# One more radix-2 step in the Fourier group's token transform, and another order of steps 11 to 14 and of the end of the heads

## The reference

```python
h = layer_norm(x, ln_in_g, ln_in_b)
for l in range(DEPTH):
    a_q, a_k, a_v, b_u, b_b, b_c, c_u, d_q, d_k, d_v = split_columns(h @ w_in[l])
    out_a = windowed_gqa_sink(a_q, a_k, a_v, sink[l])       # window 128, ALiBi, sink
    out_b = short_conv_mixer(b_u, b_b, b_c, conv_w[l])      # width 3, gated
    out_c = fourier_mixer(c_u)                              # fft2 over tokens and head width, real part
    out_d = dense_gqa(axial_rope(rms_norm(d_q)), axial_rope(rms_norm(d_k)), d_v)
    mix = concatenate([rms_norm(o, g_i) for o in (out_a, out_b, out_c, out_d)])
    h = layer_norm(DN_ALPHA * h + mix @ w_out[l], ln1_g[l], ln1_b[l])
    h = layer_norm(DN_ALPHA * h + jnp.square(jax.nn.relu(h @ w1[l])) @ w2[l], ln2_g[l], ln2_b[l])
```

## Time and profile before

| | |
|---|---|
| median of 3 runs | 1057.16 us (1056.75 to 1057.83) |
| profiled execution | 1057.18 us, span 1055.1 us |
| TensorE busy | 1038.5 us, 98% |
| VectorE, ScalarE, GpSimd busy | 761.5, 532.4, 116.8 us |
| mean granted TensorE clock | 0.998 |
| chain of waits | TensorE 94%, GpSimd 2% |

### The profile page before, as it was taken

The page is one execution under the profiler, slowest core; times in us unless marked ns, Lnnn a source line. Parts: engine busy times, 40 slices in busy tenths (PEclk is TensorE's granted clock), DMA queues, the critical chain, the costliest instruction groups (busy, mean ns, idle before and its releaser), DMA issues.

```text
span 1055.1 us, 15201 instructions
## 1 busy us (share of the span) xinstructions
PE 1038.5 (98%) x5281; PEld 868.7 (82%) x5281; DVE 761.5 (72%) x1035; ACT 532.4 (50%) x777; POOL 116.8 (11%) x122
## 2 busy tenths in 40 slices
PE   7999999999999999999999999999999999999996
PEld 6888887988888888888888888879888888888885
DVE  7845876878668757758887558677884884785787
ACT  3433666665355255355634247666634643642654
POOL 5200343200000000000002004331000000000003
PEclk9999999999999999999999999999999999999999
DMA  8432023031521521521243410311243134125122
GB/s 292 160 120 80 1 61 121 9 121 59 187 74 40 199 80 40 174 106 53 108 144 139 160 41 22 120 42 49 80 157 122 40 124 156 40 92 186 40 80 80
DMA packets 17378, 105.47 MB, mean 100 GB/s; under 512 B 2016, under 2 KB 2704, under 8 KB 5792
## 3 DMA queue, kind: packets, MB, share of 16 engines
q1 hardware_dynamic: 15984, 98.70, 26.3%
q0 software_dynamic: 1184, 5.86, 1.7%
q10 hardware_dynamic: 144, 0.07, 0.0%
HBM read 101.49 MB, written 2.10 MB: 98 GB/s over the span
## 4 chain that ended last, share of the span: by engine, by line
PE 94%; POOL 2%; issue 1%; ACT 1%; DMA 1%; DVE 0%; DVEq 0%; SPq 0%; POOLq 0%; ACTq 0%
PE bank L465 19%; PE bank L466 18%; PE bank L467 18%; PE bank L815 9%; PE bank L814 9%; PE bank L813 9%; PE bank L753 2%; PE bank L738 2%; PE bank L474 1%; PE bank L644 1%; PE bank L645 1%; POOL w_lo L1816 1%; PE bank L541 1%; POOL x L1911 1%; PE bank L548 1%
## 5 line engine op out<-in xcount | busy, mean ns | idle before, releaser
L465 PE MATMUL bank<-h_hi,w_hi 128*128 128x512 f32 (+1 forms) x688 | 257.8, 375 | 0.0
L466 PE MATMUL bank<-h_lo,w_hi 128*128 128x512 f32 (+1 forms) x688 | 257.5, 374 | 0.0
L467 PE MATMUL bank<-h_hi,w_lo 128*128 128x512 f32 (+1 forms) x688 | 257.5, 374 | 0.0
L813 PE MATMUL bank<-w_hi,hid_hi 128*128 128x512 f32 x448 | 174.4, 389 | 0.0
L815 PE MATMUL bank<-w_hi,hid_lo 128*128 128x512 f32 x448 | 174.3, 389 | 0.0
L814 PE MATMUL bank<-w_lo,hid_hi 128*128 128x512 f32 x448 | 174.3, 389 | 0.0
L1257 DVE TENSOR_TENSOR w_lo<-w_raw,w_hi 128x2048 fp32r<-128x2048 f32 x62 | 141.8, 2287 | 39.2 <-ACT w_hi L929 32.7
L929 ACT CAST w_hi<-w_raw 128x2048 fp32r<-128x2048 f32 x56 | 107.1, 1913 | 85.8 <-PE bank L815 61.5
L466 PEld LDWEIGHTS bank<-h_lo,w_hi 128*128 128x128 f32 x688 | 129.5, 188 | 23.1
L465 PEld LDWEIGHTS bank<-h_hi,w_hi 128*128 128x128 f32 x688 | 129.5, 188 | 23.0
L467 PEld LDWEIGHTS bank<-h_hi,w_lo 128*128 128x128 f32 x688 | 129.5, 188 | 23.1
(11 more groups left out here) (184 smaller groups left out, 1610.3 us busy)
## 6 DMA issues: line engine op xcount, KB each, us to landing
w_raw<-in_weights SPq DMA_DIRECT2D x63, 1024.0 KB, 4.7
w_third<-in_weights SPq DMA_DIRECT2D x23, 1024.0 KB, 4.8
rows<-in_rows POOLq DMA_DIRECT2D x4, 1024.0 KB, 4.7
w_raw<-in_weights SPq DMA_DIRECT2D x4, 512.0 KB, 8.5
out_h<-x SPq DMA_DIRECT2D x8, 256.0 KB, 2.0
x<-in_x SPq DMA_DIRECT2D x3, 512.0 KB, 9.6
dft<-in_dft SPq DMA_DIRECT2D x2, 512.0 KB, 7.0
qk_gain<-in_qk_gain POOLq DMA_DIRECT2D x3, 192.0 KB, 3.5
```

The lines of the kernel that those rows point to most:

```text
L465: pe.matmul(dst, s_hi, m_hi, start=first, stop=False)
L466: pe.matmul(dst, s_hi, m_lo, start=False, stop=False)
L467: return pe.matmul(dst, s_lo, m_hi, start=False, stop=last)
L813: pe.matmul(bank[dst + t][:], s_hi, m_hi, start=start, stop=False, skip_group_check=goes_on)
```

## The change

Three things. First, the sums for the even frequencies are folded a second time: VectorE makes them in a buffer `even` and from it the sums and differences of token n and n + 128. The frequencies 0, 4, 8, ... then need one matmul on 128 tokens, and so do 2, 6, 10, ...; each writes every second column of the bank. The columns of the table `dft` are put in that order. Secondly, in steps 11 to 14 there is one side item in each, where there were two in 11 and two in 13; and in every step `sum_quad` comes behind `turn_probs`. Thirdly, behind the last step the order is another on TensorE, ScalarE and VectorE. GpSimd's order is as it was.

```diff
--- before.py
+++ after.py
@@ -96,10 +96,10 @@
     stats=6, moments=3, row_sum=5, neg_mean=5, row_square=5, var_ready=8, rstd=8, centred=16, normed=16, rows=32,
     param=32,
     qk_gain=TOK, qk_square=TOK, dv_copied=TOK, qk_sum=TOK, qk_eps=TOK, qk_rstd=1, qk_unit=TOK,
-    rope_cos=TOK, rope_sin=2 * TOK, qk_roped=2 * TOK, tk_copied=2 * TOK, aq_hi=4, aq_lo=4, bu_copied=2,
+    rope_cos=TOK, folded_even=1, rope_sin=2 * TOK, qk_roped=2 * TOK, tk_copied=2 * TOK, aq_hi=4, aq_lo=4, bu_copied=2,
     conv_step=8, conv_out=2, group_square=4, square_added=2, square_sum=2,
     mix_hi=12, mix_lo=10, fourier_lo=2, square_mean=10, group_rstd=10,
-    qk_turned=6, k_hi=4, k_lo=4, dq_copied=2, dq_hi=4, dq_lo=2, dq_moved=32, freq=2, freq_copied=2, mixed=2, sine_copied=2, folded=2, fourier_step=4, fourier_out=2,
+    qk_turned=6, k_hi=4, k_lo=4, dq_copied=2, dq_hi=4, dq_lo=2, dq_moved=32, freq=2, freq_copied=2, mixed=2, sine_copied=2, folded=3, fourier_step=4, fourier_out=2,
     scores=UNITS, sink_put=16, biased=16, neg_max=UNITS, probs=UNITS,
     inv_denom=8, inv_widened=8, inv_turned=8, inv_copied=8, head_out=8, out_square=8, out_square_added=8, quad_sum=8, prob_turned=UNITS, prob_copied=UNITS, attended=UNITS,
     added=4 * 8 + CHUNKS * CHUNK_ADDS, relu=32, hidden_square=32, hidden_sum=16 * CHUNKS, hidden_hi=12 * CHUNKS, hidden_lo=12 * CHUNKS,
@@ -161,9 +161,10 @@
 
 SIDE_STEPS = {-1: [("s", 0)]}
 for _g in range(3):
-    SIDE_STEPS.update({4 * _g + _t: w_items(_g, _t, _t + 1) for _t in range(TOK)})
+    SIDE_STEPS.update({4 * _g + _t: w_items(_g, _t, _t + 1) for _t in range(TOK) if (_g, _t) != (2, 3)})
 SIDE_STEPS[3] = [("s", 1)] + SIDE_STEPS[3]
-SIDE_STEPS.update({13: w_items(3, 0, 1), 15: w_items(3, 1, 2), 16: w_items(3, 2, 4)})
+SIDE_STEPS.update({11: [("w", 2, 3, 0)], 12: [("w", 2, 3, 1)], 13: [("w", 3, 0, 0)], 14: [("w", 3, 0, 1)],
+                   15: w_items(3, 1, 2), 16: w_items(3, 2, 4)})
 SIDE = sum((SIDE_STEPS[_step] for _step in sorted(SIDE_STEPS)), [])
 FIRST_OF = {}
 for _step in sorted(SIDE_STEPS):
@@ -264,6 +265,7 @@
         sqd = share("sqd", [P, 2, QK])
         rope_a = share("rope_a", [P, QK])
         rope_b = share("rope_b", [P, QK])
+        even, _ = place("even", [P, 2, GROUP], F32, at=at_sqd + 4 * 2 * QK)
         freq, _ = place("freq", [P, 2, BANK], F32, at=at_sqd)
         head_square, _ = place("head_square", [P, GROUP], F32, at=at_sqd)
         inv_rows, _ = place("inv_rows", [P, GROUP], F32, at=at_sqd + 4 * GROUP)
@@ -650,12 +652,13 @@
                         scores(0)
                         scores(1)
                     wait(pe, l, "conv_step", 4 * (ct + 1))
-                    wait(pe, l, "folded", 2)
-                    for odd in range(2):
-                        c = slice(odd * SEQ // 2, (odd + 1) * SEQ // 2)
-                        for t in range(TOK // 2):
-                            last = pe.matmul(bank[4 + ct][:, c], folded[:, 2 * odd + t, ct * P:(ct + 1) * P], dft[:, t, c],
-                                             start=(t == 0), stop=(t == TOK // 2 - 1))
+                    wait(pe, l, "folded", 3)
+                    of = slice(ct * P, (ct + 1) * P)
+                    for r in range(2):
+                        pe.matmul(bank[4 + ct][:, r:HALF - 1:2], folded[:, r, of], dft[:, 0, r * P:(r + 1) * P], start=True, stop=True)
+                    c = slice(SEQ // 2, SEQ)
+                    for t in range(TOK // 2):
+                        last = pe.matmul(bank[4 + ct][:, c], folded[:, 2 + t, of], dft[:, t, c], start=(t == 0), stop=(t == TOK // 2 - 1))
                     last.then_inc(sems["freq"], 1)
 
                 wait(pe, l, "conv_out", 2)
@@ -766,26 +769,25 @@
                         take_values(p - 2)
                     if quad_scaled_in(p) is not None:
                         turn_inverse(quad_scaled_in(p))
+                    for u in pair(p - 1):
+                        turn_probs(u)
                     if quad_high_in(p) is not None:
                         sum_quad(quad_high_in(p))
-                    for u in pair(p - 1):
-                        turn_probs(u)
                 wait(pe, l, "probs", UNITS)
                 turn_half(l, 1, 0, 0)
-                take_values(PAIRS - 2)
                 for u in pair(PAIRS - 1):
                     turn_probs(u)
-                sum_quad(6)
-
-                turn_half(l, 1, 0, 1)
-                take_values(PAIRS - 1)
-                turn_inverse(7)
                 last_sides = list(sides_of(PAIRS))
                 side(last_sides[0])
                 side(last_sides[1])
-                sum_quad(7)
+                sum_quad(6)
+                take_values(PAIRS - 2)
+                take_values(PAIRS - 1)
+                turn_inverse(7)
+                turn_half(l, 1, 0, 1)
                 turn_stream(1)
                 side(last_sides[2])
+                sum_quad(7)
                 side(last_sides[3])
 
 
@@ -1119,7 +1121,7 @@
                 for u in pair(PAIRS - 1):
                     copy_turned(u)
                 copy_inverse(7)
-                stream_high_tile(0)
+                stream_high(l, 1, 0, 0)
                 def row_moments(i, t, n_added):
 
 
@@ -1137,6 +1139,7 @@
                 wait(act, l, "head_out", 8)
                 mix_high_quad(7)
                 square_head_out(7)
+                stream_high(l, 1, 0, 1)
                 stream_high_tile(1)
                 row_moments(0, 2, 30)
                 row_moments(1, 3, 32)
@@ -1460,9 +1463,12 @@
                 split_gained_half(l, 9, 0)
                 split_gained_half(l, 9, 1)
                 wait(dve, l, "tk_copied", 2 * TOK)
-                for odd, op in enumerate((ALU.add, ALU.subtract)):
-                    dve.tensor_tensor(folded[:, 2 * odd:2 * odd + 2, :], tk[:, 0:2, 0:GROUP], tk[:, 2:4, 0:GROUP], op)\
-                       .then_inc(sems["folded"], 1)
+                wait(dve, l, "qk_roped", 2 * TOK)
+                dve.tensor_tensor(even[:], tk[:, 0:2, 0:GROUP], tk[:, 2:4, 0:GROUP], ALU.add).then_inc(sems["folded_even"], 1)
+                dve.tensor_tensor(folded[:, 2:4, :], tk[:, 0:2, 0:GROUP], tk[:, 2:4, 0:GROUP], ALU.subtract).then_inc(sems["folded"], 1)
+                wait(dve, l, "folded_even", 1)
+                for r, op in enumerate((ALU.add, ALU.subtract)):
+                    dve.tensor_tensor(folded[:, r, :], even[:, 0, :], even[:, 1, :], op).then_inc(sems["folded"], 1)
 
                 for j in range(2):
                     wait(dve, l, "products", 12 + j + 1)
@@ -1623,14 +1629,15 @@
                 mix_low_quad(6)
                 normalise_first(l, 1)
                 mean_quad(6)
-                scale_quad(7)
-                stream_low(l, 1, 0)
+                low_half(l, 1, 0, 0)
                 last_sides = list(sides_of(PAIRS))
                 side(last_sides[0])
+                side(last_sides[1])
+                scale_quad(7)
                 mix_low_quad(7)
-                side(last_sides[1])
+                low_half(l, 1, 0, 1)
+                stream_low(l, 1, 1)
                 mean_quad(7)
-                stream_low(l, 1, 1)
                 side(last_sides[2])
                 side(last_sides[3])
                 k = 2 * l + 1
@@ -1988,7 +1995,7 @@
     dist = np.where(gap <= WINDOW, -gap, -1e33).astype(f32)
     turn = 2 * np.pi * (np.outer(tok, tok) % SEQ) / SEQ
     turn = turn[:SEQ // 2]
-    dft = np.concatenate([np.cos(turn[:, 0:HALF:2]), np.sin(turn[:, 2:HALF - 1:2]),
+    dft = np.concatenate([np.cos(turn[:, 0:HALF:4]), np.sin(turn[:, 4:HALF - 1:4]), np.cos(turn[:, 2:HALF:4]), np.sin(turn[:, 2:HALF:4]),
                           np.cos(turn[:, 1:HALF:2]), np.sin(turn[:, 1:HALF:2])], 1) / np.sqrt(SEQ)
     dft = dft.reshape(TOK // 2, P, SEQ).transpose(1, 0, 2).astype(f32)
     turn = 2 * np.pi * (np.outer(lane, lane) % HEAD_DIM) / HEAD_DIM
```

## The result

The changed kernel takes 1071.74 us (median of 4 runs, 1068.99 to 1073.71), the kernel before 1057.12 beside it: ratio 1.0136 [1.0111, 1.016], so 14.6 us slower. The forecast was 1063.2, its range 1060.0 to 1066.8. The sign was right, the size less than half of it, and the range missed.

The account below looks back on a forecast made before the run. TensorE, busy 98% of the span, was taken to bound the kernel. Per layer, +3.85 by the end of the heads less 0.85 for the transform gave +3.0, +6.0 in both: 1063.2 us, range 1060.0 to 1066.8.

Parts of the forecast that it names:

- granted clock 1.00 there: At the TensorE stall before the third end side, the clock was forecast to stay at its full level.
- the rival of a lower clock: Clock falls to half behind the stall before the third end side, giving 1066.2 us; chance 0.12.
- The price for one stall: Slow restart behind the end stall: 1.5 us, from the run's first 16 transposes, 3.30 us against 1.8 later.
- The transform: Smaller token transform: narrower matmuls save 0.42 us per channel half, 0.85 a layer, with VectorE's new work hidden.
- every later stage is TensorE without a gap: Whole kernel: matmul time removed or TensorE idle time added goes straight to the end.
- Step 14: Late var_eps and GpSimd's rstd ahead of its add hold up sum_quad: stall 2.5 us instead of 0.8.
- The swap in steps 4 to 10: sum_quad placed behind the transposes in these steps was forecast to cost nothing.
- step 15: Start of this step in layer 0: 181.6 instead of 180.67, +0.95 us, with step 12's gain included.
- The first gain, step 12: Side and transposes, 2.3 us of cover, remove the 0.8 us wait before sum_quad: -0.80.
- The end of the heads: New order behind the last step: hidden work begins at 203.15 instead of 199.29, +3.85 us with 0.95 from earlier.
- T: Time of turn_inverse(7) on TensorE at the end of layer 0's heads, forecast at 195.45.
- the chain behind T: From turn_inverse(7) through ScalarE and VectorE to the third end side: 4.64 us, 1.55 covered by TensorE, stall 3.1.

Follow-up runs that it names:

- g2: Changed kernel with unread matmuls filling both stalls, 18 in step 14 ahead of sum_quad(5) and 20 ahead of the third end side: 1066.23 us, ratio 1.0086.
- g1: Kernel before with the new transform alone, ScalarE's dq copies ahead of square(1) and VectorE's second mix_lo behind dk_lo: 1056.84 us, ratio 1.0.
- e3: Kernel before with sum_quad behind turn_probs and side items of steps 11 and 13 moved to 12 and 14; transform and end unchanged: 1062.79 us, ratio 1.0053.
- f1: Changed kernel with GpSimd's rstd of stream tile 0 put behind the add for quad 5 instead of ahead of it: 1066.82 us, ratio 1.0093.
- e2: Kernel before with sum_quad behind turn_probs in every step and nothing else: 1057.27 us, ratio 1.0007.
- f2: Changed kernel with h_hi and h_lo of tile 0's first half behind quad 7's mix_hi and mix_lo on ScalarE and VectorE: 1063.27 us, ratio 1.0066.
- f3: Changed kernel with 20 unread matmuls of 256 columns ahead of the third end side: 1069.09 us, ratio 1.0107.
- e4: Kernel before with the new order behind step 15 alone: 1068.56 us, ratio 1.0115.

## Why the prediction was wrong

- **The clock, the step that failed.** The sum has no term for it: "granted clock 1.00 there" was forecast, and the rival of a lower clock got 0.12, because at the end of the run the clock stands at 1.00 after 4.1 us without a matmul. That row was taken for more than it says. It shows that a stretch without matmuls reads 1.00 at first, not that a stall of 3.1 is safe. The stretches that follow it in the same trace have the fall 0.1 us later, at 1051.4, with no matmul in between (bounds, length, busy us, PEclk, DMA share, GB/s):

```profile
1051.00:1052.00 1.00, 0.00 (x0) 0.00 (x0) 0.79 (x2) 0.00 (x0) 0.02 (x1) 0.72 0.63 240
1052.00:1053.00 1.00, 0.00 (x0) 0.00 (x0) 0.62 (x1) 0.00 (x0) 0.00 (x0) 0.50 0.25 92
```

  In the changed kernel the stall read 1.00 as well (197 to 200), and the fall came when the matmuls had begun again. The price for one stall was near (1.5 taken, 1.6 measured at the end of each layer), but by luck: the row that it was taken from, the first transposes of the run, reads a clock of 1.00. It was also laid on one stall alone; step 14's has it as well in some executions. So even this rival's time, 1066.2, is 5.5 too low. g2 puts the whole at 4.8 to 5.5 us of the 14.6. The Trainium skill, "TensorE: Matmul & The Clock Gate", section "HAM oscillation — how this bites in real kernels", says that a wait between bursts can put the next at the lower clock; with 3.0 us of wait and the four microseconds behind it at 0.50 to 0.77, the trace agrees, and the rule deserved more than 0.12.
- **The transform.** -0.85 a layer by its instructions, and these are as forecast (1.31 for 1.73); -0.09 on the path. I had asked what hides VectorE's new additions, and not what is late once TensorE is early: ScalarE's copies of dq, VectorE's dk_lo, and (g1) mix_lo. This term was mis-sized as well; it is 1.5 us of the miss. The claim that every later stage is TensorE without a gap was too broad: a dense TensorE can have neighbours that are just in time.
- **Step 14.** The mechanism (var_eps late, rstd ahead of the add) was right, e3 and f1 show it. The stall was 2.9 and not 2.5, with GpSimd's two operations 0.37 longer in sum. The swap in steps 4 to 10 had been put at nothing; some 0.3 is lost before step 12. Together step 15 came 1.52 later, 0.95 forecast.
- **The first gain, step 12.** The wait vanished as forecast; e2 shows that without a side in the step most of the 0.8 is given back in the scores behind it.
- **The end of the heads.** From the start of this stretch to T it took 7.05 us, 6.90 forecast, and the chain behind T 4.75 against 4.64; stall 3.0 against 3.1. f2 shows it from the other side: two operations taken out of the chain, and the third side's wait is 0.7 or less.
- **The balance** for the profiled execution (+11.8 against +6.0): clock 3.2, transform 1.5, step 15 1.1, 0.7 in what is left of the ends and in the second layer, less 0.8 for the earlier start. Of the 2.8 up to the median, 2.1 lie in the spans (1066.8 against a median of 1068.9). They fit low clocks in further places: two of the other three runs have mean clocks of 0.992 and 0.993, and g2's small spread speaks for it. Where the clock fell in the runs without a profile isn't shown. The other 0.7 lie between span and time, and their cause is open.

## What to carry to other kernels

On an engine that is busy for 98%, price a new stall twice: its length, and the matmuls behind it at the lower clock (here 3.0 us cost 1.6 more). That an idle stretch reads 1.00 doesn't say what the work behind it will get; look at the first microsecond after one, and in each layer, since equal stalls didn't always have the same effect. Before crediting matmul time removed, read the slack of each operation that the next stage of TensorE waits for. And when a step is moved, follow what it feeds on the queues of the others, down to the instruction that stands in front there: one operation on GpSimd and one each on ScalarE and VectorE were worth 12 us here.

## What the runs showed of the hardware

- The stall of 2.7 us in step 14 lowered the clock in both layers of e3, in one layer of f2 and of f3, and in neither of the changed kernel. That of 3.0 behind 1.3 us of transposes did so in both layers of the changed kernel and of e4 and in one of f1's. Matmuls whose result isn't used held it at 1.00 (g2), and the third side came 4.75 behind L726 with them and without.
- The lower level begins at 1051.4 in the kernel before, 4.2 us after the last matmul and with none since, and in the changed kernel with the first matmul behind the stall in layer 0 and 0.7 us after it in layer 1.
- At the lower level the matmuls of 512 columns start 0.43 apart, 0.23 at the full one.
- GpSimd's operation on one column a partition took 0.70 us in one place and 0.54 in another; its add of 128x128 0.66 and 0.45. VectorE was busy throughout beside both adds.
